# A threshold search keeps its lower end and fixed numbers in the last PSUM bank, and the products beside it rotate through three bank pairs

## The reference, cut to what matters

```python
sc = jnp.einsum('bqhd,bsd->bqhs', qib, ki)
idx_score = jnp.einsum('bqhs,bqh->bqs', jax.nn.relu(sc), wib)
idx_score = jnp.where(causal[None], idx_score, -jnp.inf)
_, idx = lax.top_k(idx_score, topk)            # topk = 256
...
h = jnp.einsum('bsd,de->bse', x, w_in)         # projections: fox_q, fox_k, gate, dq, dk with rope, dv
```

## Time and profile before

| | us |
|---|---|
| median of 3 runs | 3120.19 |
| lowest, highest | 3117.55, 3122.45 |
| the profiled execution | 3115.68 |
| its span | 3114.0 |
| PE busy in it | 2840.1 |
| DVE busy | 1677.7 |
| ACT busy | 983.8 |
| POOL busy | 791.7 |
| mean granted clock of PE | 0.964 |

### The profile page before, as it was taken

One profiled execution on the slowest core, in us unless ns is written; L12 is line 12 of the kernel. 1 busy time (PEld: TensorE's weight loads), 2 busy tenths in 40 slices (PEclk: granted clock), 3 DMA queues, 4 the chain that ended last, 5 costly groups with the idle time before them and its releaser, 6 DMA issues. The chain is left out here.

```text
span 3114.0 us, 39179 instructions
## 1 busy us (share of the span) xinstructions
PE 2840.1 (91%) x14936; PEld 2311.2 (74%) x14936; DVE 1677.7 (54%) x2806; ACT 983.8 (32%) x1911; POOL 791.7 (25%) x510
## 2 busy tenths in 40 slices
PE   6999888989999999989699889989897898999988
PEld 4768678778888888868388778777684686778767
DVE  5170476534223233333999545675446998265855
ACT  3150454220000000111564034563105560244751
POOL 2233103223233333323033261003130332340021
PEclk9999899999999999999999999999899999999999
DMA  3101002111111111131122420004320224300032
GB/s 113 35 34 49 1 1 99 48 41 38 51 58 38 50 59 48 55 122 47 41 89 89 139 92 1 1 13 165 131 64 3 96 87 123 141 1 1 1 135 95
DMA packets 83146, 194.07 MB, mean 62 GB/s; under 512 B 15488, under 2 KB 34448, under 8 KB 81936
## 3 DMA queue, kind: packets, MB, share of 16 engines
q1 hardware_dynamic: 71056, 153.78, 14.6%
q10 hardware_dynamic: 11904, 37.76, 3.9%
HBM read 141.18 MB, written 33.55 MB: 56 GB/s over the span
## 5 line engine op out<-in xcount | busy, mean ns | idle before, releaser
L344 PE MATMUL psum<-H,tk_W 128*128 128x512 f32 x640 | 250.9, 392 | 23.1 <-DVE OM L2124 22.9
L344 PE MATMUL psum<-H,ffn_W 128*128 128x512 f32 x672 | 262.9, 391 | 4.8 <-DVEq L1716 3.1
L346 PE MATMUL psum<-H,ffn_W 128*128 128x512 f32 x672 | 262.4, 390 | 0.0
L345 PE MATMUL psum<-H,ffn_W 128*128 128x512 f32 x672 | 262.4, 390 | 0.0
L345 PE MATMUL psum<-H,tk_W 128*128 128x512 f32 x640 | 250.3, 391 | 0.0
L346 PE MATMUL psum<-H,tk_W 128*128 128x512 f32 x640 | 250.0, 391 | 0.0
L1930 ACT ACTIVATE MB<-OM,tk_mid 128x384 bf16<-128x384 f32 (+2 forms) x192 | 157.2, 819 | 120.7 <-DVE tk_mid L1958 119.9
L1961 DVE TENSOR_SCALAR_CACHE_REDUCE MB<-OM,tk_mid 128x512 bf16<-128x512 f32 (+2 forms) x192 | 184.3, 1010 | 2.3
L1483 POOL CAST ffn_W<-ffn_W 128x1024 fp32r<-128x1024 f32 (+1 forms) x77 | 65.1, 845 | 471.4 <-PE psum L346 469.6
L2039 POOL CAST tk_W<-tk_W 128x1024 fp32r<-128x1024 f32 (+1 forms) x56 | 53.6, 958 | 512.1 <-PE psum L346 361.0
L1697 DVE TENSOR_SCALAR ffn_Y<-ffn_G,ffn_par 128x1024 f32<-128x1024 f32 x21 | 21.1, 1004 | 288.6 <-ACT ffn_G L1670 288.6
(11 more groups left out here) (442 smaller groups left out, 7219.7 us busy)
## 6 DMA issues: line engine op xcount, KB each, us to landing
tk_W<-in_w_feat SPq DMA_DIRECT2D x40, 512.0 KB, 3.6
ffn_W<-in_ffn_w_gate SPq DMA_DIRECT2D x21, 512.0 KB, 3.5
ffn_W<-in_ffn_w_val SPq DMA_DIRECT2D x21, 512.0 KB, 3.5
ffn_W<-in_ffn_w_down SPq DMA_DIRECT2D x42, 256.0 KB, 2.6
OM<-in_w_feat SPq DMA_DIRECT2D x16, 512.0 KB, 7.7
OM<-MB ACTq DMA_DIRECT2D x64, 128.0 KB, 2.4
GATE<-OM ACTq DMA_DIRECT2D x16, 512.0 KB, 2.9
OM<-OM ACTq DMA_DIRECT2D x64, 128.0 KB, 2.9
```

What stands on the lines that cost most here:

```text
L344: pe.matmul(out, a1, b1, start=start, stop=False)
L345: pe.matmul(out, a1, b2, start=False, stop=False)
L346: return pe.matmul(out, a2, b1, start=False, stop=stop)
```

## The change

`need` and the lower end move from SBUF to PSUM, into the first columns of bank 7; the lower end has the name `low` there. The three small operations of a round read or write them there. Behind the 32 rounds one copy brings the lower end to SBUF as `lo`, for everything that follows. Since bank 7 is taken during the search, the units rotate through three pairs (banks 0 to 5), the warming matmuls write into pair 2, and the wide block, which needs all eight banks, takes its tiles in the order 4, 5, 6, 7, 0, 1, 2, 3, with its waits for the units that last used a pair set to match.

```diff
-        self.mid, self.cnt, self.need, self.keep, self.lo, self.hi = (
-            small(n, [P, 2 * N]) for n in ("mid", "cnt", "need", "keep", "lo", "hi"))
+        self.mid, self.cnt, self.keep, self.lo, self.hi = (
+            small(n, [P, 2 * N]) for n in ("mid", "cnt", "keep", "lo", "hi"))
+        self.need, self.low = (kit.psum[:, 7, 8 * n:8 * n + 2 * N] for n in range(2))
...
-        own(dve.tensor_scalar(lo, steps[:, 0:1].to_broadcast([P, 2 * N]), -1.0, None, ALU.mult))
+        own(dve.tensor_scalar(low, steps[:, 0:1].to_broadcast([P, 2 * N]), -1.0, None, ALU.mult))
...
         for i in range(BISECTIONS):
-            dve.tensor_scalar(mid, lo, steps[:, i:i + 1], None, ALU.add).then_inc(self.act_mid, 1)
+            dve.tensor_scalar(mid, low, steps[:, i:i + 1], None, ALU.add).then_inc(self.act_mid, 1)
...
             own.then(dve.tensor_tensor(keep, self.cnt, self.need, ALU.is_le))
-            own.then(dve.scalar_tensor_tensor(lo, keep, steps[:, i:i + 1], lo, ALU.mult, ALU.add))
+            own.then(dve.scalar_tensor_tensor(low, keep, steps[:, i:i + 1], low, ALU.mult, ALU.add))
+        own.then(dve.tensor_copy(lo, low))
...
-    n_pairs, SLOTS, PARTS, RING, TURNS = 4, 2, 2, len(staged), 2
+    n_pairs, SLOTS, PARTS, RING, TURNS = 3, 2, 2, len(staged), 2
+    WIDE_ORDER = (4, 5, 6, 7, 0, 1, 2, 3)
...
-                spin(kit, pe, 3, 5)
+                spin(kit, pe, 2, 5)
...
-                    for t in range(NT):
-                        if k == 0 and t % 2 == 0:
-                            pe.wait_ge(scaled, ROPES - n_pairs + t // 2 + 1)
+                    for t in WIDE_ORDER:
+                        if k == 0 and t < 6 and t % 2 == 0:
+                            pe.wait_ge(scaled, [u for u in range(U) if u % n_pairs == t // 2][-1] - COPIED + 1)
...
-                        elif t == NT - 1:
+                        elif t == WIDE_ORDER[-1]:
                             last.then_inc(products, 1)
...
-                for t in range(NT):
-                    act.wait_ge(bank_done, t + 1)
+                for n, t in enumerate(WIDE_ORDER):
+                    act.wait_ge(bank_done, n + 1)
                     act.activation(DV[:, t, :], kit.psum[:, t, :], ACT.Copy).then_inc(wide_taken, 1)
```

More of the change, by code:

```diff
@@ L1939, in search @@
         own = Own(dve, self.own_d)
-        lo, hi, mid, keep, steps, top = self.lo, self.hi, self.mid, self.keep, self.steps, self.top
+        hi, mid, keep, steps, top = self.hi, self.mid, self.keep, self.steps, self.top
+        low, lo = self.low, self.lo
         own.then(dve.tensor_reduce(top, AM[:, T0:NT], AX.X, ALU.max))
```

## The result

The changed kernel takes 3103.44 us in the median of 7 runs (3090.51 to 3105.4), the kernel before beside it 3120.19 us (7 runs, 3116.66 to 3124.44): a ratio of 0.9936, 95% interval 0.9923 to 0.995. It is faster by 0.6%, 16.7 us between the medians and some 20 us by the ratio; the forecast was 25.7 us less. The profiled executions took 3115.7 us before and 3091.3 us after (span 3089.6), 24.4 us less. One thing is needed to read these numbers: the times of both kernels fall in two groups, before at 3115 to 3121 and 3122.5 to 3126.5 us, after at 3090.5 to 3095 and 3100 to 3105 us, and both profiles shown are of the lower ones.

A forecast was written before the change was run, and what follows sets the result against it. PE sets the pace, and its wait for rope 0 in two search stages was the gain: 12.83 and 13.88 us less half a microsecond per layer, 25.7 us off 3120.2, gives 3094.5 us; range 3091 to 3107.

The forecast's parts named there:

- The bound and the gain in the stage: Search stage: PE's wait for rope 0 costs 12.83 and 13.88 us in the two layers, 26.7 us together, no more.
- POOL's hold on the small operations: Search: POOL blocks three small DVE operations with two SBUF inputs; PSUM operands free 22.4 and 23.6 us per layer.
- The price of PSUM operands: Small search operations: reading PSUM costs nothing visible, and the one write per round is taken as 0.
- The bound of 4.2 us per layer: L1966's write to PSUM: -0.13 to +0.13 us each, 4.2 us per layer either way.
- Rival (a): Search chain: PSUM operands cost 0.05 to 0.25 us per round, 2 to 7 us wait per layer, 3098 to 3109; chance 0.14.
- Three pairs: Search stage: unit 15 instead of 16 waits for rope 0, which arrives 0.8 us early in both layers; no PE wait.
- the hair: Unit 15: rope 0 only 0.8 us early, so half a microsecond per layer was allowed in the sum.
- Rival (c): Search: small operations still wait for POOL, unit 15 waits for rope 0, each layer loses one unit, 3142 us; chance 0.09.
- The order of wide banks, the warming matmuls, the added copy: Wide block and search end: new bank order and warming bank change nothing; the copy to SBUF costs 0.2 us per layer.
- the sum: Whole kernel: 12.83 and 13.88 us less, plus half a microsecond per layer: 25.7 us off the 3120.2 median, 3094.5 us.

The follow-up runs named there:

- in the copy: The changed kernel run again without any edit, with a profile: 3102.5 us (3090.77 to 3105.37), ratio 0.9927; its profiled execution took 3105.37 us.
- late ropes: The changed kernel with 30 extra six-column copies on DVE behind each search: 3114.74 us, ratio 0.997 to the kernel before.
- one-input kernel: The kernel before, four pairs, all in SBUF, its small operations per round rewritten as reductions or accumulator forms: 3097.0 us, ratio 0.9919.

## Why the prediction was right, and where it wasn't

- **The bound and the gain in the stage: right.** PE's wait for rope 0 was all there was to be had. 12.83 and 13.88 us were forecast per layer, 12.78 and 13.85 measured, the return of the clock to 1.00 included.
- **POOL's hold on the small operations: right.** All of the 22.4 and 23.6 us came free, and the two kernels with one operand in PSUM show it operation by operation. The search was forecast at 120 to 121 us and took 119.97 and 119.96. The reason given, a second SBUF input, was too narrow: L1958, held for 2.45 us, has one SBUF tensor and a pointer, so its plain form counts too. The Trainium skill, "SBUF — State Buffer", section "Who interferes with whom", has this rule (two SBUF inputs or a two-port mode contend with GpSimd). All the forms tried here agree with it, the plain copy of six columns (2.0 to 2.1 us) and the reductions (168 ns at most) too.
- **The price of PSUM operands: right at zero.** Reading -8 and -6 ns, reading and writing together +3 ns. The bound of 4.2 us per layer was far too wide; it was taken from ACT reading PSUM, for want of a row of a write. Rival (a) falls here. The Trainium skill, "VectorE: DVE Perf Modes", section "The TRN2 errata — SBUF-src ops pay a fixed extra latency per instruction", has 120 against 58 cycles; by that, an estimate from the page, the three operations would have been slower by 6.2 us per layer together, and the trace has them slightly faster.
- **Three pairs: right, and by a hair, as told.** Rope 0 comes before unit 15 is due in every stage traced: 2.0 us early in both layers of the shown execution (2580.20 against 2582.23 in the second), 0.75 us in seven of the eight stages of the others, where 0.8 us was forecast. In the shown execution the search is some 0.5 us shorter than worked out, and selection with the first multiply takes 1709.64 - 1664.38 = 45.26 us from the copy's start, against 45.82 before; in the copy it takes 46.4, so which slack comes hangs on how the selection meets POOL. Half a microsecond per layer that I had added for the hair wasn't needed. Rival (c) is what remains when the third pair stands alone, 3137.9 us; its forecast of 3142 counted the rope wait at full length and the copies of ACT at nothing.
- **The order of wide banks, the warming matmuls, the added copy: nothing,** as told; the copy takes 0.17 us.
- **The step that failed: the sum.** It took the gain of two stages off the profiled time and then off the median, and so assumed in silence that the rest of the kernel keeps its length in every execution. In the lower groups it does: 3117.8 to 3092.0 us, 25.8 less (means of all executions of each group on record, 17 and 5). In the upper groups 3124.6 became 3103.6 (33 and 11), 20.9 less, as 7.6 us more go to a lower clock in the sparse and forgetting attention of layer 1. And the median of before that the sum starts from, 3120.2 us, is of the lower group, while two executions in three of either kernel are of the upper. Over all executions the medians are 3123.9 and 3102.3 us, 21.6 apart, not 25.7. So of the 8.9 us between 3103.4 and the forecast 3094.5 some 4 us are lost in the stages behind, some 4 us come from the low start, and 1 us is spread. The gain in the stage was sized right. The range of 3091 to 3107 held the median, but it was drawn for the PSUM price, and that it also had room for these two was luck.

What stays open is why the clock falls more often there. Where PE pauses for rope 0 in the search stage (before, late ropes, one operand in PSUM, three pairs alone) no trace has the longer stages in layer 1 (90.3 to 90.5 and 78.3 to 78.4 us), and the times with late ropes keep to one group, 3113.5 to 3116.9 us. Two things speak against the pause as the cause: the shown executions of after and of the one-input kernel have no pause either and yet 90.4 and 78.3 us, and the kernel with only the lower end in PSUM, which pauses, has 95.5 us in the sparse attention of layer 2. So the longer stages of layer 1 are seen only without the pause, though not always, and no run shows why.

## What to carry to other kernels

Look at the maxima, not the medians, of tiny operations in a dependent chain, and lay the longest over GpSimd's timeline: a six-column VectorE operation can cost ten times its length, and one operand in PSUM, or a reducing or accumulating form, takes it out of the way. A buffer may be given up only as far as the late engine has been made early, so write down both times, due and there, and from more than one execution (here 2.0 us of slack in one and 0.75 in most); and a delay added or removed in a chain that another engine interrupts periodically is worth more or less than its own length. Take a gain off the profile's own execution only after a look at whether several executions of the kernel have the same stage lengths; what one stage gives, the clock may take in another.

## What the runs showed of the hardware

- VectorE operations of six columns with PSUM operands are not slower than in SBUF in a dependent chain: 224 against 231 ns, 161 against 167, 228 against 225 (input and output in PSUM).
- A small all-SBUF operation is stopped even with one input, if its form is plain (2450 ns for a `tensor_scalar`, 2061 ns for a copy of six columns); with an accumulator or as a reduction it is not (at most 223 and 168 ns, with 7 or 8 of 32 wholly under POOL's subtraction).
- Freeing one operation of a chain gave 10 us where its own excess was 4.4 and 3.3 us (8.8 and 12.8 where it was 6.0 and 5.6), and 6 us of added work became 9 to 10 us of delay: what a periodic neighbour takes from a chain depends on where it finds it.
- Executions of one kernel differ by the granted clock in stages where PE isn't full: 90.4 us at 0.96 or 95.4 us at 0.93 for the same instructions. A wait of 8.3 us in a full stage cost 10.1 to 10.5.
